# Strassen products in the pool groups of a two-layer decoder trunk

## What is computed

```
u, g = split(xn @ w_in, 2)            # xn: 256 x 2048, w_in: 2048 x 8192
for gi, w in enumerate((2, 4, 8, 16)):          # a group: 1024 columns of u and of g
    d = (csum(u) - lagged csum(u)) / count - u  # causal mean over w rows, minus u
mixed = einsum(d, w_group) * scale              # per group 1024 x 1024
h = h + (mixed * silu(g)) @ w_out               # w_out: 4096 x 2048
```

## Time and profile before

| | us |
|---|---|
| median of 3 runs | 1543.48 |
| lowest and highest run | 1542.52, 1543.58 |
| the profiled execution | 1544.08 |
| its span (what the trace shows) | 1542.0 |

### The profile page before, as it was taken

How to read it: one execution, slowest core, us unless ns; L and a number is a source line. 1 busy time by engine, 2 the same in 40 slices (tenths; PEclk the granted TensorE clock), 3 DMA queues, 4 the chain that set the end, 5 groups by cost and what they waited for, 6 DMA issues and landing times.

```text
span 1542.0 us, 19948 instructions
## 1 busy us (share of the span) xinstructions
PE 1525.7 (99%) x6788; PEld 1260.2 (82%) x6788; DVE 1114.2 (72%) x1382; ACT 935.8 (61%) x1124; POOL 28.9 (2%) x40
## 2 busy tenths in 40 slices
PE   9999999999999999999999999999999999999997
PEld 7887888888888888888888888888888888888885
DVE  6978787877878788887666675775577557755665
ACT  6466574657657574756777556644764476446853
POOL 0000000000000000000000000000000000000000
PEclk9999999999999999999999999999999999999999
DMA  9486786959678686965665757655765576555651
GB/s 382 167 257 222 223 239 218 244 171 276 220 217 244 218 219 223 242 224 198 223 220 187 219 211 219 217 196 191 218 219 189 194 221 228 210 208 180 223 195 72
DMA packets 137529, 333.11 MB, mean 216 GB/s; under 512 B 80992, under 2 KB 81008, under 8 KB 116368
## 3 DMA queue, kind: packets, MB, share of 16 engines
q1 hardware_dynamic: 132608, 314.35, 60.7%
q0 software_dynamic: 4736, 17.95, 5.8%
q10 hardware_dynamic: 144, 0.26, 0.0%
HBM read 312.08 MB, written 2.10 MB: 204 GB/s over the span
## 4 chain that ended last, share of the span: by engine, by line
PE 91%; DVE 3%; DMA 2%; issue 2%; ACT 2%; SPq 0%; ACTq 0%; POOL 0%; DVEq 0%; POOLq 0%
PE accA L515 11%; PE accA L517 11%; PE accA L516 11%; PE accC L515 10%; PE accC L517 10%; PE accC L516 10%; PE accB L515 6%; PE accB L517 6%; PE accB L516 6%; DMA w_raw<-in_stream_dram 2%; PE side L549 1%; PE side L548 1%; PE side L547 1%; DVE w_lo L1332 1%; PE accA L534 1%
## 5 line engine op out<-in xcount | busy, mean ns | idle before, releaser
L1332 DVE TENSOR_TENSOR w_lo<-w_raw,w_hi 128x1024 fp32r<-128x1024 f32 x326 | 395.8, 1222 | 226.3 <-ACT w_hi L861 224.6
L861 ACT CAST w_hi<-w_raw 128x1024 fp32r<-128x1024 f32 x326 | 340.0, 1052 | 263.2 <-PE accA L517 100.1
L1262 DVE TENSOR_TENSOR w_lo<-w_raw,w_hi 128x1024 fp32r<-128x1024 f32 (+1 forms) x280 | 320.9, 1167 | 95.4 <-ACT w_hi L874 95.4
L874 ACT CAST w_hi<-w_raw 128x1024 fp32r<-128x1024 f32 (+1 forms) x280 | 274.8, 1008 | 161.3 <-PE accA L517 79.4
L515 PE MATMUL accA<-w_hi,xa_hi 128*128 128x512 f32 x452 | 176.0, 389 | 0.8 <-DVE w_lo L1332 0.8
L517 PE MATMUL accA<-w_hi,xa_lo 128*128 128x512 f32 x452 | 175.9, 389 | 0.0
L516 PE MATMUL accA<-w_lo,xa_hi 128*128 128x512 f32 x452 | 175.9, 389 | 0.0
L515 PE MATMUL accC<-w_hi,xa_hi 128*128 128x512 f32 x396 | 154.3, 390 | 0.2 <-DVE w_lo L1262 0.2
L516 PE MATMUL accC<-w_lo,xa_hi 128*128 128x512 f32 x396 | 154.1, 389 | 0.0
L517 PE MATMUL accC<-w_hi,xa_lo 128*128 128x512 f32 x396 | 154.0, 389 | 0.0
L515 PEld LDWEIGHTS accA<-w_hi,xa_hi 128*128 128x128 f32 x452 | 84.8, 188 | 18.7 <-issue 1.1
(11 more groups left out here) (276 smaller groups left out, 2807.5 us busy)
## 6 DMA issues: line engine op xcount, KB each, us to landing
w_raw<-in_stream_dram SPq DMA_DIRECT2D x162, 1024.0 KB, 4.8
w_raw<-in_stream_dram SPq DMA_DIRECT2D x224, 512.0 KB, 5.5
w_raw<-in_stream_dram POOLq DMA_DIRECT2D x28, 512.0 KB, 8.6
h<-in_x_dram SPq DMA_DIRECT2D x4, 512.0 KB, 12.7
xT_raw<-in_xT_dram SPq DMA_DIRECT2D x3, 512.0 KB, 13.7
dec<-in_decay_dram POOLq DMA_DIRECT2D x1, 1024.0 KB, 9.1
fgain<-in_final_gain_dram POOLq DMA_DIRECT2D x1, 1024.0 KB, 7.5
out_dram<-emb SPq DMA_DIRECT2D x1, 1024.0 KB, 3.8
```

The source lines that it names most:

```text
L861: act.copy(w_hi[:, r % RING, :], w_raw[:, r // 2, (r % 2) * 1024:(r % 2 + 1) * 1024]).then_inc(hi_ready, 1)
L874: act.copy(dst, unit_raw(name)).then_inc(hi_ready, 1)
L1262: dve.tensor_tensor(w_lo[:, u % RING, 0:n], unit_raw(ORDER[u]), w_hi[:, u % RING, 0:n].bitcast(F32), ALU.subtract).then_inc(lo_ready, 1)
L1332: dve.tensor_tensor(w_lo[:, r % RING, :], w_raw[:, r // 2, (r % 2) * 1024:(r % 2 + 1) * 1024], w_hi[:, r % RING, :].bitcast(F32), ALU.subt ...
```

## The change

The three looped groups get a table of 68 units (`P_ORDER`) and a table of loads with slots (`P_LOADS`) in the manner of the heads. The first group keeps its plain order; only the banks of its last 8 units change (B and C for A and B), so that bank A is free when the loop begins.

In a looped group the two u chunks are a pair, and so are the two gate chunks. Of each pair the k tiles 8 to 15 stay plain (4 units A4 to A7, 4 units C4 to C7), and k tiles 0 to 7 go by seven products, 14 units of 6 matmuls each in place of 8 units of 12. Between them stand the output units O0 to O15 and the group product D0 to D7.

- Weight sums of the u pair are all made by DVE, 8 a group (`pool_t1`, `pool_t3`, `pool_t2`, `pool_t4`); of the gate pair 4 are made by DVE and 4 by accumulating DMAs from POOL (`group_sums`).
- ACT copies `side` three times a pair (`pool_snapshot`); DVE corrects with six instructions a pair (`pool_fix_w`, `pool_fix_c`, `pool_fix_a`).
- The four summed left operands are made in the first group (`pool_form_sum`, `pool_form_hi`, `pool_form_lo`: 11 + 4 instructions on DVE, 4 on ACT).
- DMA transposes are issued ahead of four certain loads (`P_TURNS`), the u words are joined 5 units after their halves (`P_LANDING`) and not 7, and the windows stand at units 31 to 36 and 38 to 43.
- After the loop the last mix waits in bank C (before: B), and the embedding's second product waits for it.
- 56 loads of 512 KB a group in place of 28 of 1 MB. The bytes are the same but for the 4 accumulating DMAs.

The core of the diff:

```diff
+P_ORDER = ("uA4 uM1a uA5 uM1b uA6 uM3a uA7 uM3b uC4 uM5a uC5 uM5b uC6 uM6a uC7 uM6b O0 uM7a O1 uM7b O2 uM4a O3 uM4b uM2a uM2b "
+           "O4 O5 O6 O7 O8 O9 O10 O11 O12 O13 O14 O15 gA4 gM1a gA5 gM1b gA6 gM3a gA7 gM3b gC4 gM5a gC5 gM5b gC6 gM6a "
+           "gC7 gM6b D0 gM7a D1 gM7b D2 gM4a D3 gM4b gM2a gM2b D4 D5 D6 D7").split()
+P_LOADS = (("uA4", 7, "uA4"), ("uX1a", 4, "uM4a"), ("uA5", 5, "uA5"), ("uX1b", 6, "uM4b"), ("uX2a", 2, "uM7a"), ("uA6", 0, "uA6"), ("uX3a",
...
+P_TURNS = ('uX2b', 'uC6', 'O11', 'gA5')
...
+            def group_loads(g, base):
...
+                    sp.wait_ge(lo_ready, base + (last[b] + 1))
+                    last[b] = P_AT[last_name]
...
+                    sp.dma_start(slot(b), rounds[at, s, :, half:half + UNIT * COL]).then_inc(pool_landed[b], 16)
...
+            def group_sums(g, base, p):
+
+                add_pool_block(g, base, p + "X1a", p + "X2a", p + "M1a")
+                add_pool_block(g, base, p + "X1b", p + "X2b", p + "M1b")
+                wait_pool_landed(pool, g, p + "X2a")
+                add_pool_block(g, base, p + "X2a", p + "X3a", p + "M1b")
+                wait_pool_landed(pool, g, p + "X2b")
+                add_pool_block(g, base, p + "X2b", p + "X3b", p + "M1b")
...
+            def group(g, base):
...
+                pe.wait_ge(pg_ready, n2)
+                pool_a("u", 4, base)
+                pool_part("uM1a", base, side[0][:], *a11, True)
...
+                pe.wait_ge(m_ready, n2)
+                pool_part("uM3a", base, acc["C"][0][:], *f4, True)
...
+                pe.wait_ge(mT_ready, n2)
+                mixed_out(0, base)
+                pe.wait_ge(p_snap_ready, g * 6 - 4)
+                pool_part("uM7a", base, side[0][:], *f3, False)
...
                     if c == 0 and layer == 1:
-                        pe.wait_ge(m_ready, 2 * GROUPS - 1)
+                        pe.wait_ge(pg_ready, 2 * GROUPS)
                     if c == 1 and layer == 1:
-                        pe.wait_ge(pg_ready, 2 * GROUPS)
+                        pe.wait_ge(m_ready, 2 * GROUPS)
...
+            def group_hi(g, u, base):
+
+                name = P_ORDER[u]
+                act.wait_ge(unit_used, base + (u + 1 - RING))
...
+                    if u == 5:
                         m_words(n2 - 2, g * KG - KG, 0, turn)
+                    if u == 6:
+                        m_hi(g * KG - KG, 0, turn)
+                    if u == 7:
                         m_halves(n2 - 1, 1)
+                    if u == 13:
                         m_words(n2 - 1, g * KG - KG // 2, 1, turn + 1)
+                    if u == 14:
+                        m_hi(g * KG - KG // 2, 1, turn + 1)
...
+                    group_lo(u, base)
+                    if u == 2:
+                        mix(n2 - 1, 1, "C", base)
+                    if u == 7:
                         m_lo_part(n2 - 2, g * KG - KG, 0)
+                    if u == 15:
                         m_lo_part(n2 - 1, g * KG - KG // 2, 1)
+                    if u in (4, 6):
+                        pool_t1(g, (u - 4) // 2, base)
+                    if u in (8, 9):
+                        pool_t3(g, u - 8)
+                    for i, p in enumerate(PAIRS):
+                        if u in (P_AT[p + "M5a"] + 1, P_AT[p + "M5b"] + 1):
+                            pool_t2(p, (u - P_AT[p + "M5a"]) // 2, base)
+                        if u in (P_AT[p + "M6a"] + 2, P_AT[p + "M6b"] + 2):
+                            pool_t4(g, p, (u - P_AT[p + "M6a"]) // 4, base)
+                        if u == P_AT[p + "M7b"] + 3:
+                            pool_fix_w(g * 6 - 3 + 3 * i, p_snaps[i], base + (P_AT[p + "M7b"] + 1))
+                        if u == P_AT[p + "M7b"] + 4:
+                            pool_fix_c(p_snaps[i])
+                        if u == P_AT[p + "M2b"] + 3:
+                            pool_fix_a(p_snaps[i], base + (P_AT[p + "M2b"] + 1))
```

More of the change, by code:

```diff
@@ L765, in group @@
[L765 to L772 removed]
+                pe.wait_ge(u_ready, 1)
@@ new lines, in first_group, with pool_part @@
+                pe.wait_ge(pg_ready, 2)
+                for k in range(PO_U):
+                    unit(4 * KD_U + PO_U + k, base, "C", dT_hi, dT_lo, k * UNIT, k == 0, k == PO_U - 1, seg)
+            def pool_part(name, base, bank, hi, lo, first):
+                u = P_AT[name]
+                i = "ab".index(name[3])
+                pe.wait_ge(lo_ready, base + (u + 1))
+                for b in range(UNIT):
+                    j = i * UNIT + b
+                    wh = w_hi[:, u % RING, b * COL:(b + 1) * COL]
+                    wl = w_lo[:, u % RING, b * COL:(b + 1) * COL]
+                    pe.matmul(bank, hi[:, j, :], wh, start=first and j == 0, stop=False, skip_group_check=True)
+                    pe.matmul(bank, hi[:, j, :], wl, start=False, stop=False, skip_group_check=True)
+                    mm = pe.matmul(bank, lo[:, j, :], wh, start=False, stop=j == QUADS - 1, skip_group_check=True)
+                mm.then_inc(unit_used, 1)
@@ new lines, in pool_a, with pool_c @@
+            def pool_a(p, k, base):
+                unit(P_AT[f"{p}A{k}"], base, "A", xa_hi, xa_lo, k * UNIT, k * UNIT == 2 * QUADS, k == KD_U - 1, onto=True)
+            def pool_c(p, k, base):
+                u = P_AT[f"{p}C{k}"]
+                pe.wait_ge(lo_ready, base + (u + 1))
+                for t in range(TT):
+                    mm = products(t, u % RING, "C", xa_hi, xa_lo, k * UNIT, k * UNIT == 2 * QUADS and t == 1, k == KD_U - 1, onto=True)
+                mm.then_inc(unit_used, 1)
@@ L1145, in group @@
+            def group(g, base):
+                n2 = g * 2
+                turn = POOL_TURNS - 2 + g * 4
+                for u in range(GROUP_S):
+                    group_hi(g, u, base)
+                    if u == 0:
                         m_halves(n2 - 2, 0)
-                    if not first and u == KD_U - 2:
+                    if u == 5:
                         m_words(n2 - 2, g * KG - KG, 0, turn)
+                    if u == 6:
+                        m_hi(g * KG - KG, 0, turn)
+                    if u == 7:
@@ L1640, in group @@
                             own.mark(dve.memset(b[:, :, 0:PAD], 0.0))
-                    if not first and u == 2:
-                        mix(n2 - 1, 1, "B", base)
-                    if not first and u == KD_U - 2:
+                    for i, at_u in enumerate(U_FIRST):
+                        step = u - at_u - LANDING
+                        if i == 0 and step == 0:
+                            dve.wait_ge(inv_landed, 32)
+                        if 0 <= step <= WINDOW_STEPS:
+                            window_step(0, i, step, POOL_TURNS + i)
+                        if step == WINDOW_STEPS + 1:
+                            d_lo_part(i, i)
@@ new lines, in first_group, with group @@
+                    if u == 3 * KD_U + 2:
+                        gate_p(0, 0, "A")
+                    if u == 4 * KD_U + 2:
+                        gate_p(1, 1, "C")
+                    if u in FORM_SUM:
+                        pool_form_sum(FORM_SUM.index(u), base)
+                    if u in FORM_LO:
+                        pool_form_lo(FORM_LO.index(u))
+                    if u == 4 * KD_U + PO_U + 2:
+                        mix(0, 0, "B", base + (4 * KD_U + PO_U))
+            def group(g, base):
+                n2 = g * 2
+                turn = POOL_TURNS - 2 + g * 4
+                for u in range(GROUP_S):
+                    group_lo(u, base)
+                    if u == 2:
+                        mix(n2 - 1, 1, "C", base)
+                    if u == 7:
@@ L1731, in _ @@
             dve.wait_ge(pscale_landed, 16)
-            group(0, POOL0 + MORE, True, POOL0 % 8)
-            start, steps = own.n, 2 * WINDOW_STEPS
+            first_group(POOL0 + MORE, POOL0 % 8)
+            start, steps = own.n, 2 * WINDOW_STEPS + 4
             own.n = 0
```

481 lines of the change are left out of this document (355 added, 126 removed), and 8 rows, old and new, of the table P_LOADS.

## The result

| | us, median | lowest and highest | n |
|---|---|---|---|
| before | 1543.53 | 1542.52, 1544.08 | 4 |
| the change | 1535.09 | 1533.35, 1535.29 | 4 |
| forecast | 1530.4 | range 1526.5 to 1538 | |

The ratio is 0.9947, with a 95% interval of 0.9933 to 0.9961: faster by 8.4 us. Timed again in five runs beside eleven of before it was 1535.15 against 1542.99, ratio 0.9952 [0.9939, 0.9964]. The gain is clear of noise and the time is in the range, but the gain is 4.7 us smaller than forecast. The profiled execution of the change took 1535.29, its span is 1533.2.

The account below looks back on a forecast made before the run. PE was taken to be bound by its number of matmuls. Removing 72 gives -16.3 us, plus 3.0 of waits in the groups and 0.2 after the loop: -13.1, so 1530.4 us, range 1526.5 to 1538.

Parts of the forecast that it names:

- What bounds the kernel: Looped groups: bound by the number of matmuls, 0.2266 us each, while DVE's subtractions end before PE wants the unit.
- The gain: Chunk pairs of the three looped groups: 12 matmuls fewer a pair, 72 in all, 16.3 us.
- unit 16, three groups: PE's wait at O0 in the u pair: about 0.2 us a group, from DVE's lead of -0.1 there.
- D0, three groups: Gate pair: D0's load meets the accumulating DMAs' tail, lands in 5.4 us against 4.8 of room, 0.6 a group.
- gC7, third group: Gate pair, unit 52: room of 8.6 us for its load's landing, no wait forecast.
- rounded up, 0.2 a group: Looped groups: waits of 0.2 + 0 + 0.6 us taken as 1.0 a group, 3.0 in all.
- after the loop: Second embedding product waits for the mix in bank C: 0.2 us, 0 to 1.
- the landing of O0's load: u pair: the load lands in 3.9 us against a room of 4.5, so O0 is in time.
- The walk of the u pair: Units 4 to 16, unit by unit: DVE's lead ends at -0.1 us; allowed error half a microsecond.
- A: Rival: DVE instructions don't overlap, each costs its shown time; waits 4.2 us a group, 1540.0 us; chance 0.13.
- B: Rival: accumulating DMAs delay loads at gC6, gC7, D0, D2; 7.8 us a group, 1550.6 us; chance 0.08.
- C: Rival: no wait at all, landings of 3.9 us everywhere and no error in the walk; 1527.2 us; chance 0.22.

Follow-up runs that it names:

- e7_all: The change with t4 sums one unit later, final gain's load held back, u transposes ahead of uC7's load, and uX4b and O0 exchanging slots: 1528.36 us, ratio to before 0.9901.
- e6_t4_fgain: The change with the t4 sums of both pairs one unit later and the final gain's load held until the third group's loads are through: 1530.72 us, ratio to before 0.9923.
- e3_t4_late: The change with both t4 sums of a pair one unit later, the first then behind unit 16's subtraction: 1532.89 us, one timed execution.
- e8_thin_sums: The change with DVE's 12 weight sums a group cut to 8 of 1024 columns (output not the reference's): 1530.34 us.
- e11: The kernel of e6_t4_fgain with POOL's four accumulating DMAs of a gate pair moving 64 of 1024 columns (output not the reference's): 1530.95 us.
- e2_slot: The change with uX4b and O0 exchanging load order and slots, so O0's load needn't wait for unit 13: 1536.42 us, one timed execution.
- e1_turn: The change with the second pair of u-word DMA transposes issued behind uC6's load, not ahead of it: 1533.41 us, one timed execution.

## Why the prediction was right, and where it was not

**What bounds the kernel: right.** Time goes by matmuls, and the only new waits in the groups are for `w_lo`. **The gain: right**, 72 matmuls, 16.3 us. With its waits removed the kernel is 14.6 below before. The trace of e7_all shows where the missing 1.7 lies, within the spread of executions: the groups take 441.7 us and not 440.5, of which 0.5 is at gC7 in the second group, and the loop starts 0.8 later than in the trace of before.

**The sum.** I had 3.0 + 0.2 us of waits; the profiled execution has 8.5, of which 7.2 at the named places. The terms:

| term | forecast | measured |
|---|---|---|
| unit 16, three groups | 0.6 | 4.8 |
| D0, three groups | 1.8 | 0 |
| gC7, third group | 0 | 1.9 |
| units 8 and 10, third group | 0 | 0.5 |
| rounded up, 0.2 a group | 0.6 | 0 |
| after the loop | 0.2 | 0 |

Part of the nearness is luck: 2.6 us that I had put at D0, on rounding and after the loop never came, and they cover part of what I had left out elsewhere. Without them the forecast would have been 1527.8, 7.3 off.

**The failed step is the landing of O0's load.** I found its room, 4.5 us, and that held to 0.1 us in e6_t4_fgain. Then I said that POOL moves nothing in the u pair, "so I take 3.9", from one load in a head with nothing beside it. It took 5.2 to 6.2 in one execution and 4.7 to 5.6 in another; over the 39 groups of the thirteen traces it took 3.8 to 6.4, with a median of 5.3. There is no DMA of POOL there, but SP itself issues six loads in a row in 11 us:

```profile
1093.08 11.22 SPq L505 DMA_DIRECT2D w_raw<-in_stream_dram  x6
```

The first two of them, issued 4 us apart, landed in 3.8 and 3.7 us; the other four, issued within 4.6 us, in 4.8, 5.8, 6.1 and 6.1. So loads close together land late also without POOL. That fits the rows; no run here spread them out to test it. I had named "a landing beside the transposes well over 4 us in the u pair" as what would make me wrong: the landing it was, but the one right behind the transposes was quick.

The page of the kernel before had the better number, the median landing of all its loads of this size, which I did not use (in the heads it includes loads beside accumulating DMAs, so that it fits here is in part chance):

```profile
w_raw<-in_stream_dram SPq DMA_DIRECT2D x224, 512.0 KB, 5.5
```

With 5.5 the term is 1.0 a group in place of 0.2, the forecast 1532.8.

**The walk of the u pair was a microsecond off, twice what I had allowed for it**: a lead of -0.1 at unit 16 with the t4 sum ahead of it. In the first group, where the load was not last, it was some -1.1. I had 0.9 us of DVE waiting for ACT ahead of unit 15; there were 1.3 in each group (1.33 in the rows above), and in the first 0.5 more at unit 14, since the cast of unit 12 had idled 3.14 for its own load behind the slow transposes. What I didn't do is ask which of the instructions ahead of the thin place could as well stand behind it.

**D0: wrong in the other direction.** I had put the tail of the accumulating DMAs on it. It isn't there in any group of the change; only e3_t4_late shows such a wait, beside the final gain's load. D0's loads landed in 3.9 and 5.5 us in the first two groups, and since 5.5 cost nothing either, the room is more than the 4.8 that I had.

**gC7 in the third group: missed.** I had listed what POOL issues in a gate pair and left out what stands behind it in POOL's program: the load of the final gain, which before had no accumulating DMAs ahead of it. My own rule, that each queue a step is moved past counts, would have found it.

**The rivals.** A said that DVE's instructions don't overlap at their ends. It fell: in the rows above of DVE a subtraction, a sum and a subtraction of 1.22 us each start 1.14 and 1.13 apart. The Trainium skill ("VectorE: DVE Perf Modes", The DRAIN you can't avoid) has the next instruction wait until the pipe is empty, and adds that one that isn't held starts earlier; the trace agrees with the second half alone, each starting 0.08 before the one ahead is shown as ended. A's time, 1540.0, was as far off as mine on the other side. What it had right is that DVE's amount counts at unit 16 (e8_thin_sums); what it had wrong is the price of an instruction. B's price was wrong, and of its four places only gC7 waited where the final gain's load plays no part (0.4 to 0.7 us in one group of four traces), but its mechanism is real (e11). C, no wait at all, is what e7_all nearly reaches (1528.4 against 1527.2), by four edits that the change doesn't have.

**DVE's busy time** came to 1220.6, not 1237: I had summed shown durations, and a stretch counts their overlap once.

## What to carry to other kernels

When a ring or a table of slots ties a load to the unit that frees its slot, work out the room (from that unit to the new one, less cast and subtraction) and hold it against the median landing of loads of that size under the kernel's own traffic, not against the shortest one; where they are within a microsecond, expect waits that differ from execution to execution. Before cutting work to remove a wait, look for one instruction that can stand behind the thin place and one load that can start earlier: here the two did what cutting all of DVE's weight sums did at unit 16. And when DMAs are added to an engine's program, look at what stood behind them there, in the last round of the loop above all: here an old 1 MB load cost 1.9 of the change's 8.5 us of waiting.

## What the runs showed of the chip

**PE's clock fell after a wait near 1340 us in three kernels, and not after waits of like length elsewhere.** The stretches around the wait of 2.35 us in e2_slot (the granted clock is the third number from the end):

```profile
1341.00:1343.00 2.00, 0.04 (x1) 0.05 (x1) 1.32 (x2) 1.59 (x2) 0.00 (x0) 1.00 0.37 152
1343.00:1347.00 4.00, 4.00 (x11) 3.13 (x12) 3.93 (x4) 2.00 (x2) 0.00 (x0) 0.57 0.39 136
1347.00:1351.00 4.00, 4.00 (x19) 3.29 (x18) 3.35 (x4) 2.59 (x3) 0.00 (x0) 1.00 0.66 223
```

Seven matmuls stand 0.20 us further apart than at 1.00, and those at the two ends of the stretch 0.2 more in all, so the fall to the lower level (1.2 GHz) costs 1.6 us on top of the wait. It came after waits of 1.99 (e3_t4_late), 2.31 (e8_thin_sums) and 2.35, but not after 1.86 and 2.01 in the change, and not after 2.22 at unit 16 in e1_turn:

```profile
1258.00:1260.50 2.50, 0.44 (x3) 0.10 (x1) 1.38 (x2) 2.46 (x3) 0.00 (x0) 1.00 0.02 10
1260.50:1264.50 4.00, 4.00 (x18) 3.27 (x19) 4.00 (x4) 1.92 (x3) 0.00 (x0) 1.00 0.60 189
```

So the length of the wait doesn't decide alone; what else does wasn't tried. A wait of about 2 us in the middle of full work can cost 3.6.

**The same load of the same program lands in 4.7 us in one execution and in 6.2 in another**, O0's in the third group. The nine timed executions of the change lie within 0.21% of each other all the same. In the two that were traced the waits of the groups come to 8.5 and 7.8 us: unit 16 waited 1.1 less in all in the second, and gC7 in its first group waited where it had not.
